# Stick-breaking heads as items of the block-attention pipeline, with suffix sums by reversed scans

## The reference, cut to what matters

```
z = einsum('bhqd,bhkd->bhqk', qc, k) * scale
causal = kpos[None, :] < qpos[:, None]                 # strict
sp = where(causal, softplus(z), 0.0)
tail = cumsum(sp, axis=3, reverse=True) - sp           # sum over later keys
a = where(causal, exp(log_sigmoid(z) - tail), 0.0)
out = einsum('bhqk,bhkd->bhqd', a, v)
```

## Time and profile before

| | us |
|---|---|
| runs, median of 3 (lowest to highest) | 1904.92 (1902.38 to 1909.6) |
| the profiled execution | 1902.68 |
| its span in the trace | 1900.9 |
| PE busy | 1749.1 (92%) |
| POOL busy | 764.7 (40%) |
| DVE busy | 712.1 (37%) |
| ACT busy | 701.7 (37%) |

### The profile page before, as it was taken

The page is one execution under the profiler, slowest core; times in us unless marked ns, Lnnn a source line. Parts: engine busy times, 40 slices in busy tenths (PEclk is TensorE's granted clock), DMA queues, the critical chain, the costliest instruction groups (busy, mean ns, idle before and its releaser), DMA issues.

```text
span 1900.9 us, 21440 instructions
## 1 busy us (share of the span) xinstructions
PE 1749.1 (92%) x8558; PEld 1384.3 (73%) x8558; DVE 712.1 (37%) x1466; ACT 701.7 (37%) x1284; POOL 764.7 (40%) x391
## 2 busy tenths in 40 slices
PE   6997899989978999999879978989999699999995
PEld 5886455788667888888668854558886588888884
DVE  3226873252424223211252468633323422242113
ACT  5225555353433223222343256553423422222221
POOL 4434320365143444445344443203741434444452
PEclk9999999999998999999989999999999899999998
DMA  4323100144112232222232321001431222322221
GB/s 158 110 82 100 46 1 1 56 139 138 56 67 67 89 111 89 91 108 89 69 111 89 94 67 46 1 12 67 167 110 34 67 88 92 108 89 100 100 78 56
DMA packets 100686, 154.03 MB, mean 81 GB/s; under 512 B 4284, under 2 KB 76268, under 8 KB 100588
## 3 DMA queue, kind: packets, MB, share of 16 engines
q1 hardware_dynamic: 97532, 147.16, 23.9%
q10 hardware_dynamic: 3056, 5.51, 0.9%
HBM read 150.56 MB, written 2.10 MB: 80 GB/s over the span
## 4 chain that ended last, share of the span: by engine, by line
PE 83%; DVE 9%; ACT 5%; issue 2%; POOL 1%; DMA 1%; ACTq 0%; DVEq 0%
PE banks L1255 22%; PE banks L1256 22%; PE banks L1257 22%; PE banks L1438 3%; PE banks L1456 2%; PE banks L1479 2%; PE banks L1275 1%; DVE rstd L941 1%; DVE rows L975 1%; PE banks L1639 1%; PE banks L1621 1%; PE banks L1527 1%; ACT rows L651 1%; PE banks L1530 1%; ACT proj L764 1%
## 5 line engine op out<-in xcount | busy, mean ns | idle before, releaser
L611 POOL TENSOR_TENSOR w_lo<-raw,w_hi 128x1024 fp32r<-128x1024 f32 (+1 forms) x280 | 675.2, 2433 | 924.2 <-ACT w_hi L678 924.2
L678 ACT ACTIVATE w_hi<-raw 128x1024 fp32r<-128x1024 f32 (+1 forms) x280 | 274.0, 1027 | 853.8 <-PE banks L1257 822.1
L1255 PE MATMUL banks<-w_hi,a_lo 128*128 128x512 f32 (+1 forms) x928 | 357.6, 385 | 1.4 <-ACT oT L753 1.4
L1256 PE MATMUL banks<-w_lo,a_hi 128*128 128x512 f32 (+1 forms) x928 | 355.4, 383 | 0.0
L1257 PE MATMUL banks<-w_hi,a_hi 128*128 128x512 f32 (+1 forms) x928 | 355.3, 383 | 0.0
L1255 PE MATMUL banks<-a_hi,w_lo 128*128 128x512 f32 x832 | 325.7, 391 | 0.0
L1256 PE MATMUL banks<-a_lo,w_hi 128*128 128x512 f32 x832 | 323.8, 389 | 0.0
L1257 PE MATMUL banks<-a_hi,w_hi 128*128 128x512 f32 x832 | 323.7, 389 | 0.0
L1255 PEld LDWEIGHTS banks<-w_hi,a_lo 128*128 128x128 f32 x928 | 174.7, 188 | 35.8 <-ACT oT L753 1.9
L1257 PEld LDWEIGHTS banks<-w_hi,a_hi 128*128 128x128 f32 x928 | 174.7, 188 | 34.0
L1256 PEld LDWEIGHTS banks<-w_lo,a_hi 128*128 128x128 f32 x928 | 174.7, 188 | 33.6 <-issue 0.5
(11 more groups left out here) (219 smaller groups left out, 2168.1 us busy)
## 6 DMA issues: line engine op xcount, KB each, us to landing
raw<-in_ffn_w_up SPq DMA_DIRECT2D x44, 1024.0 KB, 5.1
raw<-in_w_in SPq DMA_DIRECT2D x20, 1024.0 KB, 5.1
raw<-in_ffn_w_down SPq DMA_DIRECT2D x20, 1024.0 KB, 4.9
raw<-in_x_wk SPq DMA_DIRECT2D x8, 1024.0 KB, 5.4
raw<-in_x_wv SPq DMA_DIRECT2D x8, 1024.0 KB, 4.9
raw<-in_x_wq SPq DMA_DIRECT2D x8, 1024.0 KB, 5.1
raw<-in_x_wo SPq DMA_DIRECT2D x8, 1024.0 KB, 4.9
raw<-in_cmp_wk SPq DMA_DIRECT2D x4, 1024.0 KB, 5.4
```

Source lines behind the costliest of these rows:

```text
L611: inc(pool.tensor_tensor(w_lo[:, u % RING, n * half:n * half + n], raw[:, u % RING, n * half:n * half + n], w_hi[:, u % RING, n * half:n * ...
L678: inc(act.activation(w_hi[:, u % RING, first:first + n_half], raw[:, u % RING, first:first + n_half], ACT.Copy), hi_made)
L1255: pe.matmul(dst, st_lo, mv_hi, start=first, stop=False)
L1256: pe.matmul(dst, st_hi, mv_lo, start=False, stop=False)
```

## The change

The four stick-breaking heads become two groups of kind `sb` (pairs 6 and 7), four items each, and each item runs right behind the `sel` item of the same t: (3, sel) with (6, sb), and (4, sel) with (7, sb). There are 52 items a layer. Everything behind the pipeline that belonged to these heads (`sb_scores`, `sb_logs`, `sb_values`, `sb_softplus`, `sb_exp`, DVE's loop) goes, and so do the constants for the triangular products. Scores of an `sb` item are computed as for softmax items, queries on partitions. Its steps are: DVE adds the strict mask (from `causal`, now 8 columns wider) and copies z to SBUF, two buffers (`zb`); ACT does Abs, Exp, Ln over both halves; POOL clips z to max(z, 0) in `relu_z` (`stick_relu`, behind the Ln); DVE scans each half backwards in place, adding both; POOL subtracts that from z (`stick_log`); ACT takes the exponential one step later (`stick_exp`); transposes, copies and values are as for softmax items.

Besides: the transposes come three steps behind the scores (`LAG_T = 3`) and values a step later, two pieces a step; POOL scales both halves of softmax items, DVE only where `BY_DVE` says so; the low halves of `w_out` come at steps 6, 10, 16 and 20; `o_parts` for three of four pairs of `oT` rows are made inside the drain (order 0, 3, 1, then 2), and the output product starts on banks 0 to 5 and waits for each of the last two banks only when it comes to them.

```diff
-GROUPS = [(m, "moba") for m in range(2)] + [(m, k) for m in range(2, 6) for k in ("sel", "cmp", "win")]
+GROUPS = [(0, "moba"), (1, "moba"), (2, "sel"), (2, "cmp"), (2, "win"), (3, "sel"), (6, "sb"), (3, "cmp"), (3, "win"),
+          (4, "sel"), (7, "sb"), (4, "cmp"), (4, "win"), (5, "sel"), (5, "cmp"), (5, "win")]
-LAG_SCALE, LAG_T, LAG_V = 1, 2, 3
-PIECES = sorted((LAST[g] + LAG_V + (3 if kind == "cmp" else k), g, k)
+LAG_T = 3
+PIECES = sorted((LAST[g] + LAG_T + 1 + (1 if kind == "cmp" else k // 2), g, k)
-LO_STEPS = {6: (0, 0), 10: (0, 1), 14: (1, 0), 18: (1, 1)}
+LO_STEPS = {6: (0, 0), 10: (0, 1), 16: (1, 0), 20: (1, 1)}
...
                 def pool_scale(i):
...
+                    for hp in range(2):
+                        p, r = probs(i, hp), stat(rden, i, hp)
...
+                def stick_relu(i):
+                    pool.wait_ge(zcopied.sem, zcopied.at(l, sb_at(i)))
+                    pool.wait_ge(sb_l.sem, sb_l.at(l, sb_at(i)))
+                    inc(pool.tensor_scalar(rb(i), zb(i), 3.0e38, 0.0, ALU.min, ALU.max), relued)
+                def stick_log(i):
+                    pool.wait_ge(scanned.sem, scanned.at(l, sb_at(i)))
+                    inc(pool.tensor_tensor(both(i), zb(i), both(i), ALU.subtract), sb_d)
...
                             if i in LO_STEPS:
                                 low_half(U_OUT + LO_STEPS[i][0], LO_STEPS[i][1])
+                            if i < NI and KIND[i] == "sb":
+                                stick_relu(i)
+                            if i and SOFT[i - 1] and i - 1 not in BY_DVE:
                                 pool_scale(i - 1)
+                            if i and KIND[i - 1] == "sb":
+                                stick_log(i - 1)
...
+                    elif KIND[i] == "sb":
+                        act.wait_ge(zcopied.sem, zcopied.at(l, sb_at(i)))
+                        wait_slot(act, l, i)
+                        link(act.activation(both(i), zb(i), ACT.Abs))
+                        link(act.activation(both(i), both(i), ACT.Exp, scale=-1.0))
+                        inc(act.activation(both(i), both(i), ACT.Ln, bias=1.0), sb_l)
...
+                def stick_exp(i):
+                    act.wait_ge(sb_d.sem, sb_d.at(l, sb_at(i)))
+                    inc(act.activation(both(i), both(i), ACT.Exp), sb_p)
...
+                    if 2 <= i < NI + 2 and KIND[i - 2] == "sb":
+                        stick_exp(i - 2)
                     if 0 <= i - LAG_T < NI:
                         copy_T(i - LAG_T)
+                    if i == NI:
+                        act.wait_ge(qk.sem, qk.at(l, NI))
+                        act.wait_ge(oT_done.sem, oT_done.at(l, 6))
+                        o_parts(0)
+                        o_parts(3)
+                        o_parts(1)
...
+                    elif KIND[i] == "sb":
+                        if sb_at(i) > 2:
+                            dve.wait_ge(sb_d.sem, sb_d.at(l, sb_at(i) - 2))
+                        src = s_bank(i, 0, 1024).rearrange("p (h x) -> p h x", h=2)[:, :, 0:n]
+                        strict = causal[:, S + 1 - n:S + 1].unsqueeze(1).broadcast_to([P, 2, n])
+                        inc(dve.tensor_tensor(zb(i), src, strict, ALU.add), zcopied)
...
+                    elif KIND[i] == "sb":
+                        dve.wait_ge(relued.sem, relued.at(l, sb_at(i)))
+                        for hp in range(2):
+                            p = probs(i, hp)
+                            ins = dve.tensor_tensor_scan(p[:, ::-1], rb(i)[:, hp, ::-1], p[:, ::-1], 0.0, ALU.add, ALU.add)
+                        inc(ins, scanned)
...
-                sb_logs(0)
-                sb_scores(2)
...
-                pe.wait_ge(oT_done.sem, oT_done.at(l, 8))
-                pe.wait_ge(sb_prob.sem, sb_prob.at(l, 4))
-                rows_gemm(U_OUT, 4, 0, lambda i: pe.wait_ge(o_lo.sem, o_lo.at(l, i + 1)))
+                JO = (1, 3, 4, 4)
...
+                rows_gemm(U_OUT, 4, 0, lambda i: pe.wait_ge(o_lo.sem, o_lo.at(l, JO[i])), out_bank)
```

More of the change, by code:

```diff
@@ L78, with upto, per_half, psums @@
 XSTEPS = max(XPIECES) + 1
[L79 to L86, removed]
+def upto(kinds, i):
+    return sum(k in kinds for k in KIND[:i])
 def item_keys(i):
     return P * (ITEMS[i][1] + 1)
[L94 to L101, removed]
+def per_half(i, hp):
+    return 2 * upto(("moba", "sel", "win"), i) + upto(("cmp",), i) + hp + 1
+def psums(i, hp):
+    return 2 * i - upto(("cmp",), i) + hp + 1
+def sb_at(i):
+    return upto(("sb",), i) + 1
 def dve_scaled(i):
-    return sum(1 if CMP[j] else 1 + (j in BY_DVE) for j in range(i + 1))
-def pool_scaled(i):
-    return sum(not CMP[j] and j not in BY_DVE for j in range(i + 1))
+    return sum(KIND[j] == "cmp" or 2 * (j in BY_DVE) for j in range(i + 1))
+def pool_scaled(i, hp):
+    return sum(2 * (SOFT[j] and j not in BY_DVE) for j in range(i)) + hp + 1
 def blk_bank(b):
@@ L212, in build @@
         probT = view("probT", [P, 4, PT_ALL], F32, W)
[L213 to L217, removed]
+        relu_z = view("relu_z", [P, 2, S], F32, W + 4 * PT_ALL * 4)
+        assert 4 * PT_ALL * 4 + 2 * S * 4 <= 6 * 3968 + 2 * D * 4 and 5 * MEM * 4 + 4 * S * 4 <= 4 * PT_ALL * 4
         xb, xb_hi, xb_lo = ([view(f"{name}{i}", [P, 16 * 62], dt, W + 3968 * (3 * i + j)) for i in range(2)]
@@ L511, in turn_free, with wait_bank, wait_slot @@
         def turn_free(eng, l, i):
-            g, t = ITEMS[i]
-            turn = full_groups(g)
+            turn = TURN.index(ITEMS[i][0])
             if turn >= 2:
-                last = max(j for j in range(g) if full_groups(j) == turn - 2 and GROUPS[j][1] != "cmp")
-                eng.wait_ge(pv.sem, pv.at(l, last + 1))
+                eng.wait_ge(pv.sem, pv.at(l, PV_ORDER.index(TURN[turn - 2]) + 1))
+        def wait_bank(eng, l, i):
+            if KIND[i] == "sb":
+                eng.wait_ge(zcopied.sem, zcopied.at(l, sb_at(i)))
+            else:
+                eng.wait_ge(exped.sem, exped.at(l, per_half(i + 1, 0) - 1))
+        def wait_slot(eng, l, i):
+            if i >= PROBS:
+                eng.wait_ge(pT_psum.sem, pT_psum.at(l, psums(i - PROBS + 1, 0) - 1))
         def mem_pieces(b):
@@ L1434, in scores @@
                     else:
-                        row = {"moba": m, "sel": 4, "win": 5}[kind]
+                        row = {"moba": m, "sel": 4, "win": 5, "sb": m - 4}[kind]
                         for hp in range(2):
```

287 lines of the change are left out of this document (107 added, 180 removed).

## The result

The changed kernel takes 1917.03 us (median of 20 runs, 1911.73 to 1918.67), the kernel before 1908.38 us in the same comparison (20 runs, 1902.38 to 1915.47): ratio 1.0036, 95% interval 1.0023 to 1.0048. The medians alone would give 1.0045. The forecast of 1912 on 1904.92 was a ratio of 1.0037. The change moves a stretch of 52 us a layer off the path and gets nothing for it.

A forecast was written before the change was run, and what follows sets the result against it. PE was taken as the bound (busy 1749.1 of 1900.9 us, 83% of the chain). Per layer -39.2 + 42.4 + 1.0 - 0.5 = +3.7, twice +7.4, on 1902.68: 1910.1; with the median 2.2 higher, 1912 us, range 1888 to 1932.

The forecast's parts named there:

- Part 1: Stick-breaking stretch after the last scores: 52.2 us goes, a 13.0 us drain replaces it, gaining 39.2 us a layer.
- Part 4: Remaining effects, such as transposes three steps behind and scaling off DVE: -0.5 us a layer, bounds -2 to +1.
- Part 2: Two groups of four sb items a layer, set by their vector chain: 21.2 us a group, 42.4 a layer.
- (a) to (d): First four steps of a group, each ending with an sb item's Ln: 6.0, 5.0, 6.8 and 8.25 us.
- exit (e): Group's last step, from the last clip through scans, subtraction, Exp, copy and transposes to values: 11.45 us, the longest term.
- Rival E: In the groups, POOL scaling of 512 costs the full 0.98 us: 3.8 us more a group, 1927 us; chance 0.15.
- Part 3: PE's lower clock in the groups: 0.5 us a group, bounds 0 and 8.
- rival D: Groups' granted clock falls to about 0.7 or lower: 5 us more a group, 1930 us, throughout 1942; chance 0.14.
- B: In the groups, the scan streams at the plain pace, 2.4 us less a group: 1902 us; chance 0.14.
- C: Lag 3 hides the sb chain, PE stays the bound: groups cost 9.6 us, 1864 us, halfway 1888; chance 0.14.
- A: The forecast: sb chain sets the groups' time, scans and scalings alternating; 1912 us, range 1904 to 1922; chance 0.43.

The follow-up runs named there:

- experiment 4: Changed kernel plus two fp32 filler products on PE, computing nothing, at each of eight steps, just ahead of the transposes; ratio 0.9994.
- experiment 3: Changed kernel with pairs 6 and 7 as plain softmax items, same matmuls, without the stick-breaking computation; ratio 0.9806.
- experiment 1: Two edits of the changed kernel: POOL's scaling ahead of the clip, ratio 1.0004; clip without its wait for Ln, the scan waiting instead, 0.9967.
- Experiment 5: Two edits of the changed kernel: first three groups' values one width a step, ratio 1.0052; that plus transposes of items 0 to 13 two steps behind, 1.0011.
- experiment 2: Changed kernel with each reversed scan replaced by one plain addition of the same tiles; ratio 1.0004.

## Why the prediction was right, and where it was not

The total was right, and in part by luck. Per layer, in the two profiled executions:

| | forecast | measured |
|---|---|---|
| Part 1, the stretch that goes, less the drain | -39.2 | -40.15 |
| Parts 2 and 3, two groups with their clock | +43.4 | +43.1 |
| Part 4, the rest | -0.5 | +3.7 (early stretch +2.8, last block -0.2, elsewhere +1.1) |
| sum | +3.7 | +6.65 |

So between the two traces the change costs 13.3 us where I had 7.4. That the ratio agrees to 0.0001 is luck: the executions of before spread over 13 us, and the profiled one is from their quick end. Inside the second row two more errors cancel.

- **Part 1** held: a drain of 12.04 us in both layers instead of 13.0, a gain of 40.15 instead of 39.2.
- **Part 2** held as a mechanism, with its size 2 us too high. At the full clock (experiment 4) a group costs 42.0 - 22.85 = 19.2 us, where I had 21.2: (a) to (d) ended 1.1 us earlier in sum than my terms, the exit at full clock 0.15, and behind the third win scores came 5.75 us to the block's end where I had 4.3 + 2.2 = 6.5. That the vector chain sets it is shown by experiment 3 (9.2 us without the chain) and by experiment 1 (links taken out of it come back as time). Scans and scalings hinder each other, and undoing it gave 6 us, the 1.5 a group that I had named (in the traces the blocks shrink by 1.1 on average). That they took 3.4 us at the widest item, as I had it, is luck: both my prices were too low, and taking turns in full would have made 3.86 of the true ones. The prices: clip 1.04 for 0.98, scan 1.21 for 1.13, subtraction 2.35 as said. The scaling of 512 was too low: 0.69 with one pointer scalar, 0.77 with two, instead of 0.55. A memset was the wrong row for it. Rival E's 0.98 is no price of its own either: it was measured beside DVE's scaling, and in the kernel after it is the average over all blocks, those beside a scan included.
- **Part 3**, the clock, is the step that failed: 0.5 us a group, and it was 1.5 to 2.8. I had the bound (8) and the right pieces (PE's work on the path), but took the value from the removed stretch, whose clock was 0.93. The two score groups that I set against each other do not show what a wait does: 1.33 us of waiting stands before the slow one and before the quick one. The groups had 0.77 to 0.84, under the 0.9 that I had named as the sign of rival D. It is D's mechanism, well past its threshold of 1.1 us a group, at half its price. It was hidden because Part 2 was 2 us too high: 21.7 a group in my sum, 20.7 to 22.1 measured.
- **Part 4** failed too, and by the most: -0.5 a layer against +3.7, of which the early stretch made 1.8 us in layer 0 and 3.8 in layer 1. I looked for a price of lag and order, and costed no clock outside the groups. Experiment 5 shows a swing of 5.3 us by the clock alone. How much of the 1.8 us at 0.96 is lag 3 itself isn't settled, and before's 43.75 at a clock of 1.00 is one quick execution.
- **The rivals.** B is refuted (experiment 2), C too: PE is the bound only when the vector chain is gone (experiment 3). E is refuted as the price of every scaling. D is true in kind; its cost fell within A's range because Part 2 was too high.
- **What I would have been wrong by most.** The exit (e) was not covered by PE work. It was the longest term, and in the first group all of the clock's cost (1.5 us) lay in its last transposes and values.

What I missed altogether was that the clip waits for Ln, though it does not read the logs. I charged the clip to the path in (b), (d) and (e) without asking what it waits for.

## What to carry to other kernels

When a stretch of matrix work is replaced by a chain over in-order queues, price the chain link by link, and for each link ask which of its waits its data needs: moving one that it doesn't need was worth 13 us here, twice what a plain addition instead of the scan gave. Then price PE's own links at the lower clock level wherever waits of 1.5 to 3 us recur, also in the neighbouring stretches, and try filler work inside those waits; here it gave 8 us. A cheaper engine for one link is no gain if other engines' inputs are queued behind it.

## What the hardware showed that I had not expected

- Filler products that compute nothing made the kernel 8 us faster. Each pair of 1.98 us in the first group fitted inside a wait, and the wait's end didn't move (0.96 left of 2.87, 0.66 of 2.25).
- Identical instructions took 42.57 us at a granted clock of 1.00 and 47.88 at 0.86 in two layers of one execution.
- The reversed scan of 512 takes 1.21 us alone, 1.44 on average with POOL's scalings beside it; the plain addition of the same tiles 0.69.
- POOL's scaling of 512 takes 0.69 us with one pointer scalar and 0.77 with two; beside VectorE's scans the latter rises to 1.7 (3.42 for two).
